# Cached keys transposed in 32x32 blocks by VectorE instead of 128x128 by TensorE, in a hybrid decoder step on one core

## The reference, cut to what matters

```
def dsa_sample(q, k, v, iq, iw, ik, cache_k, cache_v, cache_idx_k, page_table, rel_bias):
    ...
    idx, valid = dsa_select(iq, iw, ik_all, q_pos, topk)
    ...
    k_sel = jnp.where(is_past, cache_k[phys, slot].astype(k.dtype), gather(k, nidx))
    v_sel = jnp.where(is_past, cache_v[phys, slot].astype(v.dtype), gather(v, nidx))
    return dsa_attend(q, k_sel, v_sel, idx, valid, q_pos, rel_bias)

def dsa_attend(q, k_sel, v_sel, idx, valid, q_pos, rel_bias):
    logits = jnp.einsum('bthd,btkhd->bthk', q, k_sel).astype(jnp.float32) * ATT_SCALE
    bias = rel_bias[rel_bucket(q_pos[None, :, None] - idx)]
    logits = logits + jnp.swapaxes(bias, -1, -2).astype(jnp.float32)
    logits = jnp.where(valid[:, :, None, :], logits, -jnp.inf)
    p = jax.nn.softmax(logits, axis=-1).astype(v_sel.dtype)
    out = jnp.einsum('bthk,btkhd->bthd', p, v_sel)
```

## Time and profile before

| | us |
|---|---|
| median of 3 runs | 1591.89 |
| lowest, highest | 1589.79, 1596.37 |
| span of the profiled execution, first to last instruction | 1593.2 |
| TensorE busy | 1471.7 (92%) |
| VectorE busy | 762.0 (48%) |
| ScalarE busy | 511.5 (32%) |
| POOL busy | 234.5 (15%) |
| mean granted clock of TensorE | 0.957 of full |

### The profile page before, as it was taken

How to read it: one execution, slowest core, us unless ns; L and a number is a source line. 1 busy time by engine, 2 the same in 40 slices (tenths; PEclk the granted TensorE clock), 3 DMA queues, 4 the chain that set the end, 5 groups by cost and what they waited for, 6 DMA issues and landing times.

```text
span 1593.2 us, 32571 instructions
## 1 busy us (share of the span) xinstructions
PE 1471.7 (92%) x13518; PEld 1334.5 (84%) x13518; DVE 762.0 (48%) x1030; ACT 511.5 (32%) x818; POOL 234.5 (15%) x371
## 2 busy tenths in 40 slices
PE   7999998979979989899998998899799999999995
PEld 4867798957867778797777998799699999999995
DVE  5288699496514540025540135543555555552123
ACT  4243223324323341023341122122344455442121
POOL 3423234154210000000000000321000110000000
PEclk8899999989999999999999999899799999999998
DMA  5415223122159979999869976133322233223221
GB/s 173 149 27 159 65 80 113 57 96 73 49 188 369 332 249 342 383 358 329 310 223 402 363 258 240 34 125 104 113 80 80 80 90 95 83 98 102 79 83 60
DMA packets 179278, 266.58 MB, mean 167 GB/s; under 512 B 20522, under 2 KB 136539, under 8 KB 178043
## 3 DMA queue, kind: packets, MB, share of 16 engines
q1 hardware_dynamic: 167947, 243.95, 44.5%
q0 software_dynamic: 5104, 11.11, 2.1%
q10 hardware_dynamic: 6080, 9.44, 1.6%
HBM read 240.28 MB, written 24.18 MB: 166 GB/s over the span
## 4 chain that ended last, share of the span: by engine, by line
PE 77%; DVE 8%; DMA 5%; ACT 3%; SPq 2%; issue 2%; POOL 2%; ACTq 0%; DVEq 0%
PE PS L987 14%; PE PS L989 13%; PE PS L988 13%; PE PS L1197 8%; PE PS L1210 4%; PE PS L1245 3%; PE PS L1319 3%; PE PS L1318 3%; PE PS L1317 3%; DMA R<-in_cache_v 3%; PE PS L1028 2%; PE PS L1029 2%; PE PS L1030 2%; PE PS L1173 1%; PE PS L1120 1%
## 5 line engine op out<-in xcount | busy, mean ns | idle before, releaser
L987 PE MATMUL PS<-xn_hi,WH 128*128 128x288 f32 (+1 forms) x1424 | 430.7, 302 | 16.0 <-DVE xn_lo L1614 13.2
L988 PE MATMUL PS<-xn_lo,WH 128*128 128x288 f32 (+1 forms) x1424 | 424.7, 298 | 0.0
L989 PE MATMUL PS<-xn_hi,WL 128*128 128x288 f32 (+1 forms) x1424 | 424.6, 298 | 0.0
L987 PEld LDWEIGHTS PS<-xn_hi,WH 128*128 128x128 f32 (+1 forms) x1424 | 271.1, 190 | 33.1 <-issue 22.2
L988 PEld LDWEIGHTS PS<-xn_lo,WH 128*128 128x128 f32 (+1 forms) x1424 | 271.9, 191 | 0.0
L989 PEld LDWEIGHTS PS<-xn_hi,WL 128*128 128x128 f32 (+1 forms) x1424 | 271.6, 191 | 0.0
L582 DVE TENSOR_TENSOR WL<-W,WH 128x2048 fp32r<-128x2048 f32 (+2 forms) x69 | 145.7, 2112 | 241.6 <-ACT WH L1358 241.6
L1358 ACT ACTIVATE WH<-W 128x2048 fp32r<-128x2048 f32 (+2 forms) x81 | 145.1, 1791 | 90.2 <-PE PS L1319 74.9
L1197 PE MATMUL PS<-CST,R 128*128 128x128 f32 x1024 | 142.7, 283 | 9.8 <-DMA R<-in_cache_k 9.5
L1793 DVE COPY RB<-PS 128x512 f32<-128x512 f32 x128 | 88.3, 691 | 115.7 <-PE PS L1197 115.7
L1197 PEld LDWEIGHTS PS<-CST,R 128*128 128x128 f32 x1024 | 112.1, 143 | 35.9 <-issue 25.7
(11 more groups left out here) (257 smaller groups left out, 2423.2 us busy)
## 6 DMA issues: line engine op xcount, KB each, us to landing
R<-in_cache_k SPq DMA_DIRECT2D x128, 512.0 KB, 5.3
R<-in_cache_v SPq DMA_DIRECT2D x128, 512.0 KB, 7.0
W<-in_w_in SPq DMA_DIRECT2D x30, 1024.0 KB, 5.4
W<-in_w_up SPq DMA_DIRECT2D x44, 512.0 KB, 4.6
W<-in_w_down SPq DMA_DIRECT2D x16, 704.0 KB, 4.4
x_scratch<-xT SPq DMA_DIRECT2D x2, 2304.0 KB, 9.0
W<-in_w_branch_a SPq DMA_DIRECT2D x4, 1024.0 KB, 7.9
W<-in_w_branch_b SPq DMA_DIRECT2D x4, 1024.0 KB, 6.1
```

Of the source, the lines that this page charges most:

```text
L987: pe.matmul(out, hi[:, k, cols], x.hi_block(n)[:, tokens], start=first, stop=False)
L988: pe.matmul(out, hi[:, k, cols], x.lo_block(n)[:, tokens], start=False, stop=False)
L989: return pe.matmul(out, lo[:, k, cols], x.hi_block(n)[:, tokens], start=False, stop=last)
```

## The change

- Cached keys no longer pass through TensorE. A page is loaded to 32 partitions: key r * 32 + k of the page goes to partition 32 * bb + k (bb is the sequence within the group) and row block r, so that a quarter of the partitions holds a sequence, and four pages (a "quad") fill the 128 partitions of a buffer KR[kp % 2]. Each DMA still has 128 rows of 4 KB. A quad is loaded in the order of quarters 0, 2, 1, 3. The eight ring buffers are the same memory and stay in use for values.
- VectorE transposes 32x32 blocks of half a quad at a time (four heads, 128x2048) into one of three buffers KTB. A partition then holds (sequence bb, dimension within a block of 32). TensorE multiplies with QB, whose 32 rows of sequence bb are nonzero only in the 8 columns of that sequence, and adds four blocks j of dimensions. The number of matmuls is unchanged: 32 for a quad.
- QB is cleared by POOL before kTn and QN, and filled by ScalarE in 32 small copies. QZ and its copies on POOL go.
- ScalarE has no evictions of keys left. VectorE runs `transposed(kp)` and then `logits(kp - 2)`.
- Both first quads are loaded ahead of 'start'. The mask's way out and back moves from SP to POOL, behind the copies and ahead of the bias terms.
- Side tiles: 'start' has 2 (3 before), each key stretch 5 (none before), each softmax 2 (1 before), the value stretches 4 and 3 (9 and 9 before), the end 1 as before. In the lists, `kl` and `o` take single banks and the side tiles alternate between the pairs; `kl` and `o` are written within one bank.

The hunks of the lists and of the reads of `o` are left out below.

```diff
@@ -148,8 +148,8 @@
     side = ([('sv', c, r) for c in range(4) for r in range(R)] + [('ga', c) for c in range(8)]
             + [('gb', c) for c in range(8)] + [('su', c) for c in range(8)])
     SIDE_B = [(1, 1), (1, 1), (1, 1), (1, 1), (1, 2), (1, 2), (1, 2), (1, 2)]
-    two, three = {7: 1, 16: 1}, {4: 1, 10: 1, 16: 1}
-    SIDE_V = [two, two, two, three, two, two, three, {4: 1, 10: 1}]
+    SIDE_K = [2, 5, 8, 11, 14]
+    SIDE_V = [{8: 1}, {8: 1}, {8: 1}, {8: 1}, {8: 1}, {8: 1}, {8: 1}, {}]
     side_at, todo = {}, list(side)
     def put_side(place, n):
@@ -158,9 +158,11 @@
     for h in range(H):
         for i in range(2):
             put_side(('B', h, i), SIDE_B[h][i])
-    put_side(('start',), 3)
+    put_side(('start',), 2)
     for G in range(2):
-        put_side(('softmax', G, 0), 1)
+        for kp in SIDE_K:
+            put_side(('K', G, kp), 1)
+        put_side(('softmax', G, 0), 2)
         put_side(('softmax', G, 1), 0)
         for b in range(4):
             for kp, n in SIDE_V[4 * G + b].items():
...
@@ -441,9 +443,10 @@
         QN = blocks(R1[:, 8192:8704], H)
         NBd = [R2[:, 4352:4608], at("NBd1", o_ikw, 256)[:, :]]
         PTs = R3[:, 0:2 * NCOL].rearrange("p (g k c) -> p g k c", g=2, k=NPG)
-        QZ = R3[:, 4352:6400].rearrange("p (h b c) -> p h b c", h=H, b=8)
+        QB = R3[:, 4352:6400].rearrange("p (g h j c) -> p g h j c", g=2, h=H, j=4)
         kTn = blocks(R3[:, 6400:7424], H)
-        KTb = [blocks(RB[:, 1024 * i:1024 * i + 1024], H) for i in range(2)]
+        KR = [blocks(R1[:, 4096 * i:4096 * i + 4096], 4) for i in range(2)]
+        KTB = [blocks(a, 4) for a in (RB[:, 0:2048], R3[:, 0:2048], R3[:, 2048:4096])]
         SV = blocks(R1[:, 4608:9728], 5)
         SG = R3[:, 0:1024]
@@ -551,11 +554,15 @@
                 if seq == 4:
                     e.wait_ge(S_("ring_free"), 1)
                 return
-            G, kind, n = (seq - 8) // 128, (seq - 8) // 64 % 2, (seq - 8) % 64
-            if kind == 0:
-                e.wait_ge(single_filled, single.slots['kp', G, n, 1][0] + 1)
+            G, kind, n = seq // 128, seq // 64 % 2, seq % 64
+            if kind == 0 and n >= 8:
+                e.wait_ge(S_("k_transposed"), 32 * G + 2 * (n // 4 - 1))
+            elif kind == 0:
+                e.wait_ge(S_("v_pages_used"), 64 * G - 4 + 4 * (n // 4))
+            elif n < 8:
+                e.wait_ge(S_("k_transposed"), 32 * G + 30 + 2 * (n // 4))
             else:
-                e.wait_ge(S_("v_pages_used"), 64 * G + n + 1)
+                e.wait_ge(S_("v_pages_used"), 64 * G + n - 7)
         def next_chunk(tile):
@@ -705,26 +712,33 @@
                 if seq >= 256:
                     return
                 G, kind, n = seq // 128, seq // 64 % 2, seq % 64
-                b, kp = (4 * G + n % 4, n // 4) if kind == 0 else (4 * G + n // 16, n % 16)
                 page_freed(sp, seq)
-                v = page_id(sp, b, kp)
-                sp.dma_start(ring[seq % 8], (cache_k, cache_v)[kind][0, bass.ds(v, 1)]
-                             .rearrange("o p h d -> (o p) (h d)")).then_inc(page_in[seq % 8], 16)
+                if kind == 0:
+                    bb, kp = n % 4, n // 4
+                    v = page_id(sp, 4 * G + bb, kp)
+                    sp.dma_start(KR[kp % 2][32 * bb:32 * bb + 32, :, :],
+                                 cache_k[0, bass.ds(v, 1)].rearrange("o (r k) h d -> k (o r) (h d)", r=4))\
+                        .then_inc(page_in[seq % 8], 16)
+                else:
+                    v = page_id(sp, 4 * G + n // 16, n % 16)
+                    sp.dma_start(ring[seq % 8], cache_v[0, bass.ds(v, 1)].rearrange("o p h d -> (o p) (h d)"))\
+                        .then_inc(page_in[seq % 8], 16)
+            def load_quad(seq):
+                for i in ((0, 2, 1, 3) if seq // 64 % 2 == 0 else range(4)):
+                    load_page(seq + i)
+            load_quad(0)
+            load_quad(4)
             side_loads('start')
-            for seq in range(4):
-                load_page(seq)
-            sp.wait_ge(S_("sample_mask"), 1)
-            sp.dma_start(mask_scr, S).then_inc(S_("mask_out"), 16)
-            sp.wait_ge(S_("mask_out"), 16)
-            for j in range(4):
-                sp.dma_start(MG[32 * j:32 * j + 32, :], mask_scr[0:32, :]).then_inc(S_("mask_in0"), 16)
-            for seq in range(4, 8):
-                load_page(seq)
             for G in range(2):
-                for n in range(64):
-                    load_page(128 * G + n + 8)
+                for kp in range(NPAGES):
+                    load_quad(128 * G + 4 * kp + 8)
+                    if kp:
+                        side_loads('K', G, kp - 1)
+                side_loads('K', G, NPAGES - 1)
                 side_loads('softmax', G, 0)
                 side_loads('softmax', G, 1)
                 for b in range(4):
@@ -894,15 +908,16 @@
             drained(pool, 'pv', H - 1)
             pool.wait_ge(S_("k_stored0"), 48)
             pool.wait_ge(S_("k_stored1"), 32)
+            pool.memset(QB, 0.0).then_inc(S_("queries_cleared"), 1)
             link(pool.memset(kTn[:, :, TS:P], 0.0))
             link(pool.tensor_copy(kTn[:, :, 0:TS], kT[:, :, TP:T]))
             link(pool.tensor_copy(QN, qT[:, :, TP:T]))
             pool.memset(ST[0:1, 110:111], 0.0).then_inc(S_("ring_free"), 1)
-            link(pool.memset(QZ, 0.0))
-            for b in range(NB_):
-                c = b % 4
-                last = pool.tensor_copy(QZ[:, :, b, 8 * c:8 * c + 8], qT[:, :, TP + 8 * b:TP + 8 * b + 8])
-            last.then_inc(S_("sample_queries"), 1)
+            pool.wait_ge(S_("sample_mask"), 1)
+            pool.dma_start(mask_scr, S).then_inc(S_("mask_out"), 16)
+            pool.wait_ge(S_("mask_out"), 16)
+            for j in range(4):
+                pool.dma_start(MG[32 * j:32 * j + 32, :], mask_scr[0:32, :]).then_inc(S_("mask_in0"), 16)
             pool.wait_ge(S_("sample_queries"), 1)
             pool.wait_ge(S_("nbr_in"), 16 * 32)
             pool.wait_ge(S_("stored_pool"), 32)
@@ -1186,37 +1201,29 @@
             sides('start')
             for G in range(2):
-                for n in range(65):
-                    if n < 64:
-                        seq = 128 * G + n
-                        pe.wait_ge(page_in[seq % 8], 16 * (seq // 8 + 1))
-                        for u in range(2):
-                            claim(pe, 'kp', G, n, u)
-                            for i in range(4):
-                                h = 4 * u + i
-                                last = pe.transpose(bank('kp', G, n, u)[:, P * i:P * i + P],
-                                                    ring[seq % 8][:, HD * h:HD * h + HD], ident)
-                            done(last, 'kp', G, n, u)
-                    if (G, n) == (0, 1):
+                for kp in range(NPAGES):
+                    if (G, kp) == (0, 0):
                         pe.wait_ge(S_("sample_queries"), 1)
-                    if n:
-                        kp, bb = (n - 1) // 4, (n - 1) % 4
-                        if bb == 0:
-                            claim(pe, 'kl', G, kp)
-                        for u in range(2):
-                            drained(pe, 'kp', G, n - 1, u)
-                            for j in range(4):
-                                h = 4 * u + j
-                                last = pe.matmul(pbank('kl', G, kp)[32 * j:32 * j + 32, u, 0:P],
-                                                 QZ[:, h, 4 * G + bb, :], KTb[(n - 1) % 2][:, h, :],
-                                                 start=(bb == 0), stop=(bb == 3))
-                        if bb == 3:
+                    claim(pe, 'kl', G, kp)
+                    for u in range(2):
+                        pe.wait_ge(S_("k_transposed"), 32 * G + 2 * kp + u + 1)
+                        keys = KTB[(2 * kp + u) % 3]
+                        for j in range(4):
+                            for c in range(4):
+                                last = pe.matmul(bank('kl', G, kp)[32 * c:32 * c + 32, P * u:P * u + P],
+                                                 QB[:, G, 4 * u + c, j, :],
+                                                 keys[:, :, P * c + 32 * j:P * c + 32 * j + 32],
+                                                 start=(j == 0), stop=(j == 3))
+                        if u == 0:
+                            last.then_inc(S_("k_half_used"), 1)
+                        else:
                             done(last, 'kl', G, kp)
+                    sides('K', G, kp)
                 claim(pe, 'kl', G, NPG - 1)
                 for u in range(2):
                     for j in range(4):
                         h = 4 * u + j
-                        last = pe.matmul(pbank('kl', G, NPG - 1)[32 * j:32 * j + 32, u, 0:P],
+                        last = pe.matmul(bank('kl', G, NPG - 1)[32 * j:32 * j + 32, P * u:P * u + P],
```

(51 more changed lines are left out.)

25 lines of the change are left out of this document (13 added, 12 removed).

## The result

The changed kernel takes 1679.07 us (median of 4 runs, 1676.63 to 1680.04) against 1590.84 (1589.04 to 1596.37): ratio 1.0545, 95% interval 1.052 to 1.057. It is 88 us slower, where 37 were predicted; 1679 lies outside the range of 1538 to 1670.

A forecast was written before the change was run, and what follows sets the result against it. TensorE was taken to bound the key stretches before, page transfers to 32 partitions after. Keys +26 and +51, values -50 and softmax +11 gave +38; 37 added to the median made 1629 us, range 1538 to 1670.

The forecast's parts named there:

- my own case: Key stretches: page transfers bind at 232 to 280 GB/s; total 1629 us, own range 1600 to 1648, chance 0.35.
- What bounds a key stretch, (c): Key stretches: page transfers to 32 partitions at 248 GB/s, 2.11 us a page, 8.4 us a quad, set the pace.
- the 6% rule: Key stretches: using both halves gains only 6% over 219 GB/s: 232 GB/s, 2.26 us a page, total 1648 us.
- The sum of group 0's keys: First key stretch: pages, chunks, stores, mask and tail end it at 606.5 us against 580.7, +26 us.
- Group 1's keys: Second key stretch: pages, three chunks, five stores, tail and start take 157.4 us against 106.6, +51 us.
- Values: Value stretches with fewer tiles: transfers bound them, 83 and 78 us against 110.0 and 101.3, -50 us.
- Softmax: Both softmax stretches: a second side tile delays the values, +5.5 us twice, 11 us.
- (a) transposes: VectorE in key stretches: 2.29 us per 128x2048 transpose; two transposes and the logit additions make 5.3 us a quad.
- (b): Key stretches: the cycle of two quad buffers takes 12.1 us for two quads, 6.1 us each.
- the halves overlap: Key stretches: engines write both halves at once, rate returns to 419 GB/s; -55 us, 1537 us, chance 0.34.
- Lock step: Key stretches: all engines stay on the same half, 2.39 us a page, +36 us, 1665 us; chance 0.20.
- the slow transposes: Key stretches: VectorE transposes take 4.58 us, 10.4 us a quad; sum +74 us, 1666 us; chance 0.06.

The follow-up runs named there:

- experiment 2: Changed kernel with the four pages of a quad loaded in the order of quarters 0, 1, 2, 3 instead of 0, 2, 1, 3: 1692.69 us, ratio 1.0635.
- experiment 9: Changed kernel with its seven side tiles of the value stretches moved to the end of the kernel: 1692.91 us, ratio 1.0634.
- experiment 10: Changed kernel with the seven side tiles of the value stretches moved into the key stretches: 1654.36 us, ratio 1.0399.
- Experiment 1: Changed kernel with each cached key page sent to all 128 partitions of one row block, keys in wrong places: 1597.53 us, ratio 1.0037.
- the wide kernel: Changed kernel with whole key pages to 128 partitions by one row block instead of 32 by four: 1597.53 us, ratio 1.0037.

## Why the prediction was wrong

The direction was right, and so was the mechanism of my own case for the key stretches: the transfers bind them, for the reason given. Two terms were too small, the rate of a key page and the value stretches; with either miss alone the time would have stayed in the range. In the order of the prediction's steps:

- *What bounds a key stretch, (c).* This step failed: "I take 248: 2.11 us a page". Measured were 223 to 228 GB/s for pages alone, 2.30 to 2.35 us: 0.19 to 0.24 a page, 12 to 15 us in each group, 24 to 31 of the 48 that the stages missed by. The 248 was read in two microseconds around one change of half; I priced every page as if it were all border. The whole row at 219, 2.39 us, has one change of half in the bytes of two pages, as experiment 2 has; one more for every second page is worth 0.11 a page by that experiment, which gives 2.28. The sum by the 6% rule, 1648, had the rate nearly right (232).
- *The sum of group 0's keys*, 17 us short: 12 to 15 by the rate, and 4 because three weight chunks went among its pages (issued at 455.85, 532.68 and 593.64), where the sum had two; a quad with a chunk took 13.2 us, 3.8 more. The start was right. The third quad was transposed only at 485.43, after 10.9 us of waiting, since the mask copies and a chunk stood among its pages, but the sum's own terms give the same with the measured rate: 444.3 + 2 + 12 x 2.33 + 3.8 + 7.6 = 485.7. VectorE's timeline of the changed kernel:
```profile
458.37 2.31 DVE L1825 STREAM_TRANSPOSE RB<-R 128x2048 f32<-128x2048 f32 x1
...
470.04 2.31 DVE L1825 STREAM_TRANSPOSE R<-R 128x2048 f32<-128x2048 f32 x1 [7.17 <-DMA R<-in_cache_k]
...
485.43 4.50 DVE L1825 STREAM_TRANSPOSE R<-R 128x2048 f32<-128x2048 f32 x2 [10.88 <-DMA R<-in_cache_k]
...
746.72 2.31 DVE L1825 STREAM_TRANSPOSE RB<-R 128x2048 f32<-128x2048 f32 x1 [10.94 <-DMA R<-in_cache_k]
```
- *Group 1's keys*, 12 short: 12 to 15 by the rate, less 4, since two chunks (785.25, 846.36) went among its pages and not three. The first quad is transposed 10.6 us after the values end (last row); the sum had 9.4 for that, 1 and four pages of 2.11.
- *Values*, 10 and 13 us short, together nearly as large a miss as the rate, and the other step that failed. Here the mechanism was wrong: I took the larger of TensorE's and the queue's work (56 pages, chunks and stores at full rate), as if the smaller hid behind it. With a ring of eight pages neither engine runs through: pages alone take 79 us (experiment 9), where 56 x 1.25 + 2.3 = 72 were taken, and a tile adds 3.6. (That 79 + 4 x 3.6 = 93 and 78 + 3 x 3.6 = 89 come near the 92.0 and 90.0 is no test, since the 3.6 is the mean of these two differences.)
- *Softmax*, priced 4.6 us too high: the second tile cost 3.6 and 2.8 us, not 5.5.
- *(a) transposes*: 2.29 us taken, 2.27 to 2.31 measured. Right. *Logits* in runs of 32: right; at full clock half a quad takes 1.08 us, four pages 2.2, as before. TensorE's timeline of the changed kernel:
```profile
527.54 1.08 PE L1213 MATMUL PS<-RB,R 128*32 128x128 f32 x32
```
- *Tiles in TensorE's idle time* of the keys: right, even for nine (experiment 10). *The clock* fell as said, to 0.71 to 0.73 of full in the mean of the key stretches; no run isolates its cost.
- *(b), and with it the rival "the halves overlap".* Had the rate been 419, the prediction said 1537. Experiment 1 is that case: 1597.5. The cycle of two buffers takes 7.6 to 8.1 us a quad, not 6.1, and holds the queue to 299 to 313 GB/s. In its rows the transposes of one buffer end at 504.5 and the next in it start at 515.08, 10.6 us for issuing and landing four pages, where I had put down 7.45 (0.3 + 2.85 + 4.3, the 4.3 chosen below a row that said 5.3; in the wide kernel a page lands 5.6 us after its issue in the median). Of the 0.36 for faster, 0.34 stood on this term.
- *Lock step.* Its two rates, 219 and by the 6% rule 232 GB/s, lie on either side of the measured 223 to 228. Its time with 219 (1665), and that of the slow transposes (1666), came within 14 us of 1679, but in part by luck: the one has pages a little slower than measured, the other transposes of 4.58 us, and both have the value stretches 23 us too short.

## What to carry to other kernels

Before a tile is reshaped so that another engine can work on it, price its transfer in the new shape: here 132 us of TensorE's transposes were bought with 1 us more for each of 128 page transfers, because the 32 partitions of a page lie in one half. Price the cycle of the buffers too: with full-width pages the change still gained nothing (1597.5 us), since two quad buffers gave a quad only every 7.6 us, four pages at 1.9, where TensorE had taken 1.60 for a page. Take a rate from a whole row, not from its best two microseconds. Where a ring is short and a block of other work holds the consumer until the transfers under way have landed or beyond, the stretch costs more than the larger of the two works: here each tile added 3.6 us to a stretch of values. The same seven tiles cost nothing that could be seen in the key stretches, where TensorE stood idle for over 40% of the time before the move.

## What the runs showed of the hardware

Key pages in rows of 4 KB on one queue, with a few weight chunks and stores among them, moved at 230 to 235 GB/s into partitions of one half, whether 32 or 64 of them (221 to 223 when the half changed only at every second page), and at 297 to 312, with the engines at 0.86 to 0.88, when 32 partitions were spread over both. Pages alone into one half moved at 223 to 228, and at 212 to 214 when the half changed only at every second page. A cut of a one-sided page into two transfers changed nothing (1678.5 against 1679.1 us). Two queues that each fed one half reached 250 to 278 GB/s, more than the alternation on one. A 32x32-block transpose of 128x2048 in f32 took 2.27 to 2.31 us, as much as a subtraction of the same size, and 1.20 to 1.25 at half the size.
